# Attention's band packed into 128 columns a head: one transpose a head and a second product on masked probabilities

## What is computed

```python
dist = ATTN_BLOCK + qi - kj
band = (dist >= 0) & (dist < WINDOW)          # WINDOW = ATTN_BLOCK = 128
s = jnp.where(mask[None, :, None, None], s, -jnp.inf)
m = jnp.maximum(jnp.max(s, axis=-1, keepdims=True), sink)
p = jnp.exp(s - m)
denom = jnp.sum(p, axis=-1, keepdims=True) + jnp.exp(sink - m)
o = jnp.einsum('bnhgqk,bnkhd->bnqhgd', (p / denom).astype(v.dtype), vv)
```

## Time and profile before

| what | value |
|---|---|
| runs | 1841.97, 1844.21, 1845.28 us; median 1844.21 |
| profiled execution | 1842.9 us, of which the span from first to last instruction is 1841.1 |
| granted TensorE clock | 0.995 over the span |
| busy share of the span | PE 98%, weight loads 82%, DVE 70%, ACT 54%, POOL 29% |
| chain that ended last | PE 91%, DVE 3%, issue 2%, ACT 1%, DMA 1%, POOL 1% |
| attention | about 276 to 536 us and 1037 to 1286 us |

### The profile page before, as it was taken

The page is one execution under the profiler, slowest core; times in us unless marked ns, Lnnn a source line. Parts: engine busy times, 40 slices in busy tenths (PEclk is TensorE's granted clock), DMA queues, the critical chain, the costliest instruction groups (busy, mean ns, idle before and its releaser), DMA issues.

```text
span 1841.1 us, 29466 instructions
## 1 busy us (share of the span) xinstructions
PE 1799.2 (98%) x10368; PEld 1508.8 (82%) x10368; DVE 1287.9 (70%) x2628; ACT 986.9 (54%) x2127; POOL 536.1 (29%) x857
## 2 busy tenths in 40 slices
PE   6999999999999999989999999999999999999999
PEld 4788888888878888868888888887888887888887
DVE  7966467777766566678546677775775557987987
ACT  5622226877775665542322577877656555343341
POOL 1000026777723323300002467763333221000000
PEclk9999999999999999999999999999999999999999
DMA  9143232222223344344143322131432238378352
GB/s 354 69 160 108 99 119 88 74 73 63 58 96 98 107 140 127 112 152 155 48 147 108 108 74 73 36 88 33 169 107 75 64 129 291 118 250 286 110 177 92
DMA packets 158497, 222.36 MB, mean 121 GB/s; under 512 B 11792, under 2 KB 104336, under 8 KB 150672
## 3 DMA queue, kind: packets, MB, share of 16 engines
q1 hardware_dynamic: 158352, 220.49, 35.8%
HBM read 163.18 MB, written 57.28 MB: 120 GB/s over the span
## 4 chain that ended last, share of the span: by engine, by line
PE 91%; DVE 3%; issue 2%; ACT 1%; DMA 1%; POOL 1%; SPq 0%; DVEq 0%; POOLq 0%; ACTq 0%
PE bank L889 71%; PE bank L1046 3%; PE bank L1035 3%; PE bank L1067 3%; PE bank L1128 2%; PE bank L1100 2%; PE bank L1115 2%; PE bank L1093 1%; PE bank L999 1%; PE bank L1142 1%; DMA g_raw<-in_w_in 1%; PE bank L1117 1%; PE bank L1084 0%; DMA raw<-in_w_in 0%; PE bank L1002 0%
## 5 line engine op out<-in xcount | busy, mean ns | idle before, releaser
L889 PE MATMUL bank<-h_hi,w_hi 128*128 128x512 f32 x512 | 206.6, 403 | 0.2
L889 PE MATMUL bank<-h_lo,w_hi 128*128 128x512 f32 x512 | 199.9, 390 | 0.0
L889 PE MATMUL bank<-h_hi,w_lo 128*128 128x512 f32 x512 | 199.6, 390 | 0.0
L889 PE MATMUL bank<-wq_hi,h_hi 128*128 128x384 f32 x512 | 176.9, 346 | 0.5 <-issue 0.5
L889 PE MATMUL bank<-ob_hi,oa_hi 128*128 128x512 f32 x448 | 175.0, 391 | 0.0
L889 PE MATMUL bank<-ob_hi,oa_lo 128*128 128x512 f32 x448 | 174.4, 389 | 0.0
L889 PE MATMUL bank<-ob_lo,oa_hi 128*128 128x512 f32 x448 | 174.3, 389 | 0.0
L889 PE MATMUL bank<-wq_hi,h_lo 128*128 128x384 f32 x512 | 172.0, 336 | 0.0
L889 PE MATMUL bank<-wq_lo,h_hi 128*128 128x384 f32 x512 | 171.3, 334 | 0.0
L1310 ACT ACTIVATE g_hi<-g_raw 128x2048 fp32r<-128x2048 f32 x36 | 68.9, 1915 | 165.2 <-PE bank L889 155.9
L1465 ACT ACTIVATE sm<-sm,neg_m 128x257 f32<-128x257 f32 x256 | 127.4, 504 | 18.0 <-DVE neg_m L2025 18.0
(11 more groups left out here) (254 smaller groups left out, 4838.4 us busy)
## 6 DMA issues: line engine op xcount, KB each, us to landing
g_raw<-in_w_in SPq DMA_DIRECT2D x24, 1024.0 KB, 6.1
raw<-in_w_in SPq DMA_DIRECT2D x16, 1024.0 KB, 7.9
o_lower<-mixed_cols SPq DMA_DIRECT2D x32, 512.0 KB, 6.2
nat_rows<-u SPq DMA_DIRECT2D x48, 256.0 KB, 2.6
raw<-in_w_in SPq DMA_DIRECT2D x8, 1536.0 KB, 6.7
o_upper<-in_w_out SPq DMA_DIRECT2D x24, 512.0 KB, 8.2
wa<-in_w_ada SPq DMA_DIRECT2D x8, 1024.0 KB, 10.8
g_q<-gate_cols SPq DMA_DIRECT2D x64, 128.0 KB, 2.5
```

The lines of the kernel that those rows point to most:

```text
L889: mm = pe.matmul(dst, a, b, start=(first and m == 0), stop=(last and m == 2), **more)
```

## The change

The band is packed: column k of a head holds the score with the previous block's key where k > q and with the own block's key where k <= q. ACT first copies the previous block's scores (all -1e30 in the very first block of a group, from `no_prev`) into `sm`; DVE then writes the own block's scores over them where the int32 mask `own` is set, with four `copy_predicated`, and takes the maximum of all four heads with one `reduce_max`. Exponentials and scalings have 129 and 128 columns. PE makes one transpose a head, all four into one bank. ACT alone copies them out; DVE multiplies the copy with the mask `prev_T` into `pTm`. The product with V is own V times `pT` plus `vd` times `pTm`, where `vd` is the previous block's V less the own one's, made by DVE once a block. The number and the size of the matmuls with V stay. On DVE `qn` goes ahead of the scores. The scores' bank is free with `own_ok` (the maximum included) in place of `masked_ok`. The large mask load is replaced by two smaller ones that count on `const_in`, for which `lower_bounds` now waits.

```diff
@@ PE att_iter
-                    if j >= 1:
-                        pe.wait_ge(pta_ok, S + j)
-                        pe.wait_ge(ptv_ok, S + j)
+                    if j >= 2:
+                        pe.wait_ge(pta_ok, S + j - 1)
                     for h in range(GH):
-                        for half in range(2):
-                            at = ((h % 2) * 2 + half) * P
-                            mm = pe.transpose(bank[5 + h // 2][:, at:at + P],
-                                              sm[j % 2][:, h, half * P:(half + 1) * P], ident[:])
+                        mm = pe.transpose(bank[5 + j % 2][:, h * P:(h + 1) * P], sm[j % 2][:, h, 0:P], ident[:])
...
-                    for half in range(2):
+                    for v, p_T in ((vv[:, j % NBLK + 1, :], pT), (vd[:, j % NBLK, :], pTm)):
                         for e in range(2):
-                            mm = pe.matmul(bank[7][e * HD:(e + 1) * HD, 0:2 * P], vv[:, j % NBLK + half, :],
-                                           pT[j % 2][:, e:GH:2, half, :], start=(half == 0), stop=(half == 1))
+                            mm = pe.matmul(bank[7][e * HD:(e + 1) * HD, 0:2 * P], v, p_T[j % 2][:, e:GH:2, :],
+                                           start=(p_T is pT), stop=(p_T is pTm))
...
-                        pe.wait_ge(masked_ok, (GH + 1) * (S + j))
+                        pe.wait_ge(own_ok, (GH + 2) * (S + j))
@@ ACT att_iter, at its head
+                if 3 <= b <= ATT_B + 2:
+                    j = b - 3
+                    act.wait_ge(s_ok, S + j + 1)
+                    if j >= 2:
+                        act.wait_ge(pt_ok, S + j - 1)
...
+                    for e in range(2):
+                        src = bank[2 + e][:, :].rearrange("p (a c) -> p a c", a=2)[:, :, 0:P]
+                        act.activation(sm[j % 2][:, e:GH:2, 0:P],
+                                       no_prev[:].unsqueeze(1).to_broadcast([P, 2, P]) if first else src, ACT.Copy
+                                       ).then_inc(prev_ok, 1)
...
-                        act.activation(sm[j % 2][:, h, 0:2 * P + 1], sm[j % 2][:, h, 0:2 * P + 1], ACT.Exp,
+                        act.activation(sm[j % 2][:, h, 0:P + 1], sm[j % 2][:, h, 0:P + 1], ACT.Exp,
...
-                        a = act.activation(sm[j % 2][:, h, 0:2 * P], sm[j % 2][:, h, 0:2 * P], ACT.Identity,
+                        a = act.activation(sm[j % 2][:, h, 0:P], sm[j % 2][:, h, 0:P], ACT.Identity,
...
-                    act.activation(pT[j % 2][:, 0:2, :, :].rearrange("p h a q -> p (h a q)"), bank[5][:, :],
-                                   ACT.Copy).then_inc(pta_ok, 1)
+                    act.activation(pT[j % 2][:].rearrange("p h q -> p (h q)"), bank[5 + j % 2][:, :], ACT.Copy
+                                   ).then_inc(pta_ok, 1)
@@ DVE att_iter: the part on the scores goes behind qn
-                    waits = [(s_ok, S + j + 1)]
+                    waits = [(prev_ok, 2 * (S + j + 1))]
...
-                    for h in range(GH):
-                        dve.tensor_tensor_reduce(sm[j % 2][:, h, 0:2 * P],
-                                                 bank[2 + h % 2][:, (h // 2) * 2 * P:(h // 2 + 1) * 2 * P],
-                                                 mask, 1.0, NEG, ALU.add, ALU.max,
-                                                 row_max[:, h:h + 1]).then_inc(masked_ok, 1)
+                    for h in range(GH):
+                        at = (h // 2) * 2 * P + P
+                        dve.copy_predicated(sm[j % 2][:, h, 0:P], own[:], bank[2 + h % 2][:, at:at + P]).then_inc(own_ok, 1)
+                    dve.wait_ge(own_ok, (GH + 2) * (S + j) + GH + 1)
+                    dve.reduce_max(row_max, sm[j % 2][:, :, 0:P], AX_X).then_inc(own_ok, 1)
...
+                if 1 <= b <= ATT_B:
+                    j = b - 1
+                    if s > 0 and j % NBLK == 0:
+                        dve.wait_ge(carry_in, 48 * (j // NBLK + 1))
+                    if j >= NBLK:
+                        dve.wait_ge(pv_ok, S + j - NBLK + 1)
+                    dve.tensor_tensor(vd[:, j % NBLK, :], vv[:, j % NBLK, :], vv[:, j % NBLK + 1, :], ALU.subtract)
...
-                    dve.wait_ge(pt_ok, S + j + 1)
-                    if j >= 2:
-                        dve.wait_ge(pv_ok, S + j - 1)
-                    dve.tensor_copy(pT[j % 2][:, 2:4, :, :].rearrange("p h a q -> p (h a q)"),
-                                    bank[6][:, :]).then_inc(ptv_ok, 1)
+                    dve.wait_ge(pta_ok, S + j + 1)
+                    dve.tensor_tensor(pTm[j % 2][:], pT[j % 2][:],
+                                      prev_T[:].unsqueeze(1).to_broadcast([P, GH, P]), ALU.mult).then_inc(ptv_ok, 1)
@@ constants
-            for dst, src in ((masks[:], masks_d), (causal[:], causal_d)):
-                sp.dma_start(dst, src).then_inc(late_in, 16)
+            for dst, src in ((own[:], own_d), (prev_T[:], prev_d), (causal[:], causal_d)):
+                sp.dma_start(dst, src).then_inc(const_in, 16)
```

More of the change, by code:

```diff
@@ L74, in hybrid_layer @@
 def hybrid_layer(nc, x, cT, pos, norm_w, w_ada, b_cols, b_gate, w_in, qk_w, sinks, rec_w, lbT, w_out,
-                 ident_d, masks_d, causal_d, freq_d, out, mixed_T, nat, gate_T, x_T_d, a21_d, carry_k, carry_v):
+                 ident_d, own_d, prev_d, causal_d, freq_d, out, mixed_T, nat, gate_T, x_T_d, a21_d, carry_k, carry_v):
     with ExitStack() as ctx:
@@ L86, in hybrid_layer @@
         state = keep("state", [P, RHEADS, RK])
-        masks = keep("masks", [P, 2, 2 * P])
+        own = keep("own", [P, P], I32)
+        prev_T = keep("prev_T", [P, P])
+        no_prev = keep("no_prev", [P, P])
         mod_a = keep("mod_a", [P, KT])
@@ L177, in hybrid_layer @@
         sizes = [("kT_hi", [P, NBLK + 1, P], F32R), ("kT_lo", [P, NBLK + 1, P], F32R)]
-        sizes += [(f"pT{i}", [P, GH, 2, P], F32) for i in range(2)]
+        sizes += [(f"{n}{i}", [P, GH, P], F32) for n in ("pT", "pTm") for i in range(2)]
         sizes += [("vv", [P, NBLK + 1, HD], F32), ("row_max", small, F32)]
@@ L189, in hybrid_layer @@
         at_slot(20480, 24576, [("sq", wide, F32), ("qn", wide, F32), ("rc", wide, F32)])
-        at_slot(24320, 32768, [(f"sm{i}", [P, GH, 2 * P + 4], F32) for i in range(2)])
+        at_slot(24320, 32768, [(f"sm{i}", [P, GH, P + 4], F32) for i in range(2)] + [("vd", [P, NBLK, HD], F32)])
         at_slot(32768, 34816, [("rs", wide, F32), ("q_ss", small, F32), ("q_var", small, F32), ("q_rinv", small, F32)])
@@ L200, in hybrid_layer @@
         q_ss, q_var, q_rinv = [named[n][:, 0:GH + 1] for n in ("q_ss", "q_var", "q_rinv")]
-        q_rot, k_rot, qT_hi, qT_lo, sm, pT, o_mix = [[named[f"{n}{i}"] for i in range(2)] for n in
-                                                     ("q_rot", "k_rot", "qT_hi", "qT_lo", "sm", "pT", "o_mix")]
+        vd = named["vd"]
+        q_rot, k_rot, qT_hi, qT_lo, sm, pT, pTm, o_mix = [[named[f"{n}{i}"] for i in range(2)] for n in
+                                                     ("q_rot", "k_rot", "qT_hi", "qT_lo", "sm", "pT", "pTm", "o_mix")]
         kT_hi, kT_lo, vv, no_key = [named[n] for n in ("kT_hi", "kT_lo", "vv", "no_key")]
@@ L252, in hybrid_layer @@
         const_in = sem("const_in")
-        late_in = sem("late_in")
         const_ok = sem("const_ok")
@@ L289, in hybrid_layer @@
         t_ok, thi_ok, tcopy_ok = sem("t_ok"), sem("thi_ok"), sem("tcopy_ok")
-        s_ok, masked_ok, max_ok, exp_ok = sem("s_ok"), sem("masked_ok"), sem("max_ok"), sem("exp_ok")
+        s_ok, prev_ok, own_ok, max_ok, exp_ok = sem("s_ok"), sem("prev_ok"), sem("own_ok"), sem("max_ok"), sem("exp_ok")
         rden_ok, pn_ok = sem("rden_ok"), sem("pn_ok")
@@ L1434, in att_iter @@
                 S = s * ATT_B
+                if 3 <= b <= ATT_B + 2:
[3 more added lines that the diff above has]
+                        act.wait_ge(pt_ok, S + j - 1)
+                    first = s == 0 and j % NBLK == 0
+                    if first:
+                        act.wait_ge(const_ok, 4)
+                    for e in range(2):
[3 more added lines that the diff above has]
+                                       ).then_inc(prev_ok, 1)
                 if b == ATT_B + 1:
@@ L2378, in _ @@
                 if s == 0:
-                    dve.wait_ge(late_in, 32)
+                    dve.wait_ge(const_in, 16 * 11)
+                    dve.memset(no_prev[:], NEG)
                     dve.memset(vv[:, 0, :], 0.0)
@@ L2523, in constants @@
     q, k = np.arange(P)[:, None], np.arange(P)[None, :]
-    prev = np.where(k > q, 0.0, NEG)
-    own = np.where(k <= q, 0.0, NEG)
-    first = np.concatenate([np.full((P, P), NEG), own], 1)
-    later = np.concatenate([prev, own], 1)
-    masks = np.stack([first, later], 1).astype(np.float32)
+    own = (k <= q).astype(np.int32)
+    prev_T = (q > k).astype(np.float32)
     s, t = np.arange(P)[:, None], np.arange(P)[None, :]
@@ L2532, in constants @@
     sign = np.tile(inv, (P, 1))
```

(6 more changed lines are left out.)

28 lines of the change are left out of this document (13 added, 15 removed).

## The result

The changed kernel takes **1850.41 us** (median of 9 runs, 1848.44 to 1854.08), the kernel before 1843.69 us beside it (9 runs, 1840.73 to 1845.28): a ratio of 1.004, 95% interval 1.003 to 1.005. The profiled execution took 1850.68 us with a span of 1848.8, against 1842.9 and 1841.1 before. The forecast was 1848, slower being its likeliest sign.

A forecast was written before the change was run, and what follows sets the result against it. PE bound the kernel; after the change a ring of ACT and DVE would. Per segment: turns +1.8, head +1.5, slack -1.1, iterations 32 and 33 -0.87, tail +1.1, together +2.4, +4.9 for both: 1847.8, said 1848; range 1826 to 1864.

The forecast's parts named there:

- PE's saving: In attention on PE: four transposes fewer save 0.435 us a block, 7.46 to 7.03 us an iteration.
- The ring: In attention, ACT and DVE wait for each other by turns: 7.20 us plain, 7.76 with weights, 8.14 large.
- POOL's half hold: Half of the possible delay of DVE's product by POOL's q_rinv: 0.09 us a plain turn, 0.05 with weights.
- my turns: Forecast ring turns to b=31 a segment: 16 plain, 9 with weights, 2 large, 203.3 us against PE's 201.5.
- What POOL adds: In attention, POOL's q_rinv may hold DVE's product up to 0.17 us plain, 0.11 with weights; 0.09 and 0.05 taken.
- PE's 7.03 as a floor of each turn: In attention: a plain turn of 7.20 us already lies above PE's own iteration of 7.03 us.
- Head and slack: Per segment: first block's scores behind qn, +1.5 us (0 to 2.7); ring running later against PE, -1.1 us.
- The drain: Tail from b=34 to the end of the last product with V: +1.1 us a segment, between 0 and 2.5.
- The sum's own last step: From the profiled execution, forecast at 1847.8 us, to the median, 1.3 above it; the forecast said 1848.
- (1): Rival: PE stays the bound in attention, saving 24 us, 1819; chance 17%.
- (2): Rival: the ring binds, but its turns are 0.1 to 0.3 us shorter than counted, 1832 to 1843; chance 15%.
- (3): Rival: DVE's sink copy waits some 0.7 us behind POOL's rc every turn, +38, 1886; 15% with milder forms.

The follow-up runs named there:

- the kernel with four transposes: The kernel before with only the own half's transposes, four a block instead of eight, leaving out the previous block's share: 1816.19 us.
- the weights' low part later: The changed kernel with DVE's subtraction for the low part of the next weights moved from ahead of r_den to behind q_ss: 1836.39 us.
- the logarithm first: The changed kernel with ACT's logarithm of the forget gate ahead of the copies of the last block's scores: 1852.91 us.
- the scores first: The changed kernel with DVE's part for the scores ahead of qn again, as before the change: 1838.91 us.
- its edits: The kernel before with its low-part subtraction behind q_ss, 1843.36 us, or with only the own half's transposes, 1816.19 us.
- products first: The changed kernel with the products with V ahead of the transposes on PE and o_mix ahead of the masked product on DVE: 1830.76 us.
- both edits: The changed kernel with two reorderings: products with V ahead of transposes (o_mix ahead of the masked product), and the weights' low part behind q_ss: 1828.10 us.
- PE's work given back: The changed kernel with four more unused transposes of the identity a block on PE, behind the products with V: 1855.17 us.
- drain alone: The changed kernel with products with V ahead of transposes, o_mix ahead of the masked product, for a segment's last two blocks only: 1848.66 us.
- filled wait: The changed kernel with 14 unused transposes of the identity on PE in the wait ahead of a segment's last products with V: 1847.99 us.

## Why the prediction was right, point by point

- **PE's saving.** 0.435 a block, 7.03 us an iteration: shown by the kernel with four transposes (7.015 a turn, -27.4 us). PE's busy time fell by 24.2 us, not by the 28 forecast; the fall of the clock, which lengthens matmuls, is part of the difference.
- **The ring.** Its parts and its order are those of the sum: product at 0.62 (forecast 0.62), `neg_m` started at 3.74 (3.79), `sq` at 5.65 (5.57), next copy at 7.24 (7.20, 7.29 with POOL's half hold). With weights 7.91 (7.76, or 7.81), with the large pieces 8.18 (463.39 to 479.75 holds two; 8.14, or a little more). The 26 turns came to 195.4, against 196.0 by my turns. That each price taken from a far row (`rg_w` for the product, `a_T` for the predicated copies, `q_ss` and 128 columns for `reduce_max`) was within 0.01 us of a piece is what made the sum hold.
- **What POOL adds** was about the right size for the wrong reason, which is luck. `q_rinv` ran from 388.09 for 1.18 us while the product started at 388.94 and took its bare 0.69, so it holds nothing off. What POOL's rotation held, because `qn` and with it the rotation start earlier now, are `neg_m` (+0.15) and `g_q` (+0.18 on the earlier trace rows). The exclusive lock that the Trainium skill states ("SBUF — State Buffer", the section on its two separate sides) agrees with these two rows (`neg_m` ends at 392.37, POOL's `rc` beside it at 392.35) and with the last product of a segment, 1.27 us beside POOL's `k_inv`; the row of `q_rinv` doesn't, and there the measurement decides.
- **PE's 7.03 as a floor of each turn**, with which I called a plain turn "already above" it: only the mean counts. Here nothing hung on it, since the mean was above too.
- **Head and slack** were both too small and mostly cancel, which is luck too. The ring started 1.5 late, 2.8 counted from attention's own start (forecast 1.5), and PE used 2.2 of slack against it (forecast 1.1): ACT's copy at b = 31 is 2.86 later than before, PE's start of b = 32 only 0.64 (506.49 and 507.13).
- **The drain** is the step that was mis-sized: forecast +1.1, measured +1.9, and +4.6 in segment 2. ACT's first exponential of the last block, before and after:

```profile
526.45 0.49 ACT L1465 ACTIVATE sm<-sm,neg_m 128x257 f32<-128x257 f32 x1
```

```profile
528.17 0.39 ACT L1476 ACTIVATE sm<-sm,neg_m 128x129 f32<-128x129 f32 x1
```

From PE's start of b = 34 to this exponential it is 1.9 more (forecast 2.1: the ring is later against PE, and the copies stand ahead of the loads), from there to ACT's next copy 0.86 less (forecast 0.9), and from that copy to the last products with V 0.84 more (forecast 0.6). So the mechanism of the sum is there. Its three sizes add up to 1.8; it came to +1.1 only because the wait of 0.74 that was there before was counted as slack. It was none: PE waited there for the end of this same chain, so all that was added to the chain came out. And a fall of the clock, 2.7, was not in the sum at all.
- **The total.** The profiled execution grew by 7.8 where +4.9 was forecast; without the fall it would be +5.1, with the drain's other 1.6 and the preamble's -1.3 nearly cancelling, again by luck. The sum's own last step, 1.3 from the profiled execution to the median, would have given 1849, not 1848.
- **Rivals.** PE is not the bound (1), though with the two reorderings it is; turns were not shorter (2); the sink copy took 0.16 each time and the predicated copies 0.30 as in the earlier trace rows, `rc` never went first (3).

## What to carry to other kernels

Work taken off the bound engine pays only if the chain that replaces it closes in less time than that engine's turn, so write down the whole circle of the engines that now wait for each other, not the busy times: PE went from 98% to 96%, and the time rose by 0.4%. Then look for pieces in the circle that needn't be there: two reorderings without a new buffer or instruction turned +0.4% into -0.8%. And compare the engine beside the ring with the mean of the ring's turns, not with each, where it runs a piece ahead; and measure its need again when the order changes (7.015 became 7.15 here with the same matmuls).

## What the runs showed of the hardware

TensorE's granted clock fell to its lower level (1.2 of 2.4 GHz) in a drain in which PE was busy for most of the time: its waits just before were 0.80 and 1.92 us, with 1.08 us of matmuls between them. For 5.9 us the matmuls of 512 columns took 0.63 instead of 0.39 us. Nearly the same waits in segment 1 of the same execution left the clock at 1.00. Over the profiled executions of this study: where the last wait of a drain was 1.91 or 1.92 us (the changed kernel, the weights' low part later, the logarithm first, the scores first), the clock fell in 6 of 8 drains; where the longest was 1.46 or less (before, with or without its edits, products first, both edits, PE's work given back, drain alone, filled wait), in none. So the fall was seen only with such a wait, and not with each; with the wait filled it stayed away in both drains of one profiled execution. What decides in the two drains without a fall stays open. The timed runs give only each run's mean granted clock: 0.9931 on average with the scores first, 0.9941 for the changed kernel, 0.9950 with the filled wait, 0.9947 for the kernel before in the same round. A fall of 5.9 us to half the clock is 0.0016 of the span, so these agree with about one fall a run in the first and about one in every second run of the changed kernel. That is an estimate, and from small differences.

Two kinds of operation that POOL holds were not expected either: a `neg_m` of 4 columns went from 0.16 to 0.31 us and `g_q` of 256 from 0.52 to 0.84 (0.43 alone, in the drain at 528.29) when the start of `qn` moved POOL's rotation beside them, with no change in what they do. It goes the other way too: with both edits POOL's `q_var` of 5 columns took 0.77 instead of 0.20 beside DVE's subtraction.

The order of PE's pieces has a price. One turn of the same matmuls takes PE 7.015 us with the four transposes behind the projection (the kernel with four transposes) and 7.15 with them behind the products with V (both edits). Why is open.
